# Hybrid decoder layer with 32 experts, one core: gather two tiles ahead at the end of a step, tile loops written out

## What is computed

```python
logits = xf @ w_router + b_router
top_v, top_i = lax.top_k(logits, 4)
gates = softmax(top_v)
# tokens sorted by expert, each expert's rows cut into blocks
hmid = xblk @ w_up[e] + b_up[e]                # 1024 -> 2048
hg = minimum(hmid[:, :1024], 7.0)
hl = clip(hmid[:, 1024:], -7.0, 7.0)
act = hg * sigmoid(1.702 * hg) * (hl + 1.0)
yb = act @ w_down[e] + b_down[e]               # 1024 -> 1024
y = segment_sum(yb * gate, token)
```

## Time and profile before

| what | us |
|---|---|
| median of the runs | 1562.85 |
| the profiled execution, its span | 1565.7 |
| TensorE busy with matmuls | 1300.1 (83%) |
| VectorE busy | 530.9 (34%) |
| ScalarE, GpSimd busy | 209.8, 225.4 |
| share of 16 DMA engines taken by the loads, stores of SyncE's queue | 77.3% |
| weights of the experts | 256 issues of 1024 KB and 256 of 512 KB |

### The profile page before, as it was taken

How to read it: one execution, slowest core, us unless ns; L and a number is a source line. 1 busy time by engine, 2 the same in 40 slices (tenths; PEclk the granted TensorE clock), 3 DMA queues, 4 the chain that set the end, 5 groups by cost and what they waited for, 6 DMA issues and landing times.

```text
span 1565.7 us, 30929 instructions
## 1 busy us (share of the span) xinstructions
PE 1300.1 (83%) x11087; PEld 697.0 (45%) x11088; DVE 530.9 (34%) x1344; ACT 209.8 (13%) x561; POOL 225.4 (14%) x349
## 2 busy tenths in 40 slices
PE   7999999999898977669998996695796886857865
PEld 5778777778786532223443332231232332312322
DVE  2999756643573251111211111111111111111155
ACT  2111232414240210000000000000000000000001
POOL 2008700124220010000100000000010000001320
PEclk9999999999999998779999997898898998978987
DMA  7586455204037789999978999999999999999996
GB/s 186 125 267 158 101 128 143 86 9 109 1 119 230 279 364 419 420 410 416 419 290 357 405 417 418 419 419 416 419 419 417 406 390 412 418 417 419 418 372 237
DMA packets 147329, 480.52 MB, mean 307 GB/s; under 512 B 15438, under 2 KB 76118, under 8 KB 114471
## 3 DMA queue, kind: packets, MB, share of 16 engines
q1 hardware_dynamic: 135695, 463.37, 77.3%
q0 software_dynamic: 2560, 10.29, 1.6%
q10 hardware_dynamic: 9024, 6.17, 1.2%
HBM read 462.42 MB, written 18.21 MB: 307 GB/s over the span
## 4 chain that ended last, share of the span: by engine, by line
PE 59%; DMA 17%; DVE 8%; issue 6%; SPq 3%; POOL 3%; ACT 2%; DVEq 1%; POOLq 0%
PE bank L1287 17%; DMA arena<-in_w_up 16%; PE bank L1299 10%; PE bank L782 9%; PE bank L1255 5%; PE bank L1273 3%; DVE acc L1826 3%; PE bank L1174 2%; PE bank L1182 2%; PE bank L865 2%; POOL acc L548 2%; SPq L447 2%; SPq L450 1%; PE bank L1082 1%; POOL temps L545 1%
## 5 line engine op out<-in xcount | busy, mean ns | idle before, releaser
L1287 PE MATMUL bank<-arena,gate 128*32 128x512 f32 x3264 | 420.0, 643 | 125.4 <-DMA arena<-in_w_up 124.8
L1287 PEld LDWEIGHTS bank<-arena,gate 128*32 128x32 f32 x3264 | 103.9, 113 | 395.8 <-issue 270.7
L782 PE MATMUL bank<-arena 128*128 128x304 f32 (+1 forms) x1024 | 263.9, 420 | 3.7 <-DMA arena<-in_w_in 2.2
L2368 DVE COPY gate<-bank 128x256 f32<-128x256 f32 x46 | 19.6, 425 | 634.9 <-PE bank L1299 634.9
L782 PEld LDWEIGHTS bank<-arena 128*128 128x128 f32 x1024 | 196.9, 193 | 68.2 <-ACT zs L1497 3.1
L1299 PE MATMUL bank<-arena,gate 128*32 128x256 f32 x3264 | 190.5, 384 | 30.9 <-ACT gate L1717 29.3
L1299 PEld LDWEIGHTS bank<-arena,gate 128*32 128x32 f32 x3264 | 112.4, 111 | 96.7 <-issue 27.1
L1826 DVE SCALAR_TENSOR_TENSOR acc<-arena,pcol,acc x240 | 126.3, 609 | 0.1
L672 POOL TENSOR_TENSOR qkv<-qkv 128x192 f32<-128x192 f32 x46 | 29.4, 639 | 613.3 <-DVE qkv L2312 613.3
L1273 PE MATMUL bank<-qkv 128*128 128x512 f32 x102 | 59.5, 666 | 49.9 <-DVE gate L2354 23.4
L1255 PE MATMUL bank<-qkv 128*32 128x256 f32 (+1 forms) x1224 | 87.2, 401 | 2.0 <-POOL qkv L675 1.2
(11 more groups left out here) (424 smaller groups left out, 1169.7 us busy)
## 6 DMA issues: line engine op xcount, KB each, us to landing
arena<-in_w_up SPq DMA_DIRECT2D x256, 1024.0 KB, 12.7
arena<-in_w_down SPq DMA_DIRECT2D x256, 512.0 KB, 8.6
arena<-in_w_in SPq DMA_DIRECT2D x32, 1024.0 KB, 10.4
y_d<-gate ACTq DMA_DIRECT2D x188, 32.0 KB, 4.9
y_d<-gate POOLq DMA_DIRECT2D x1, 4608.0 KB, 28.3
arena<-in_w_conf_out SPq DMA_DIRECT2D x4, 1024.0 KB, 5.1
arena<-in_state_dn_S SPq DMA_DIRECT2D x8, 512.0 KB, 7.3
arena<-in_w_dn_out SPq DMA_DIRECT2D x1, 4096.0 KB, 15.2
```

The lines of the kernel that those rows point to most:

```text
L782: last = mm(bank[2 * (j % 2) + f][:, 0:cols.stop - cols.start], wring[:, slot, k, P * half:P * (half + 1)], rhs[:, k, cols], start=(k == 0 ...
L1287: last = mm(hidden(q)[v], xgT[:, i, SL * q0:SL * (q0 + 1)], parts(wup[k], q)[v], start=False, stop=(k == KC - 1), skip_group_check=True)
```

## The change

- The two halves of bank 0 are taken apart: the turned rows go to the right half of bank 6 (`xgt_bank`), so VectorE reads them there.
- In a step, the gather moves from after up chunks 0 to 3 to the end, and it is that of tile b+2, not b+1. The turn of tile b+1's rows moves from the end to just after the turn of the activation, before down. It gets a wait for `y_ready`. In the last four steps the gather stands at the end too, in the first two of them.
- ScalarE's order becomes `copy_actt(b-1)`, `store_y(b-1)`, `sigmoid(b)`, `copy_xg(b+2)`.
- No loop over tiles stays on TensorE, ScalarE, VectorE and GpSimd. Tiles 2 to 27 are written out, then 35 steps each inside the condition of the one before (`nx > b - FIXED`), then the last four. Tile numbers are constants but in the last four. The gates are now turned before tile 28.
- VectorE no longer makes the table of tile numbers (12 or so small operations). SyncE's loop stays.

```diff
             def tile_step(b):                       # TensorE
                 up_bias(b)
                 up(b, range(0, 4), now_in)
-                gather(b + 1)
                 turn(act_h, bank[4], s["act_ready"], b, s["actt_done"])
+                if not first(prev):
+                    pe.wait_ge(s["y_ready"], prev)
+                turn(xg, xgt_bank, s["xg_copied"], b + 2, s["xgt_done"])
                 down(prev, range(KC), prev_in)
                 up(b, range(4, KC), now_in)
-                turn(xg, bank[0][:, W:2 * W], s["xg_copied"], b + 2, s["xgt_done"])
+                gather(b + 2)
...
-            with pe.Fori(2, HEAD) as b:
+            for b in range(2, FIXED):
                 tile_step(b)
             turn_gates()
             pe.wait_ge(s["mask_ready"], 3)
             nx = pe.value_load(info_i[0:1, 0:1], min_val=0, max_val=XB)
-            with pe.Fori(0, MID) as i:
-                b = pe.value_load(info_i[0:1, bass.ds(i + O_MID, 1)], min_val=0, max_val=XB + MID) + HEAD
-                tile_step(b)
-                with pe.Fori(0, EXTRA) as j:
-                    with pe.If(i + j * MID < nx):
-                        tile_step(b + j + 1)
+            with ExitStack() as more:
+                for b in range(FIXED, FIXED + XB):
+                    more.enter_context(pe.If(nx > b - FIXED))
+                    tile_step(b)
...
             def tile_step(b):                       # ScalarE
-                copy_xg(b + 1)
                 copy_actt(b - 1)
+                store_y(b - 1)
                 sigmoid(b)
-                store_y(b - 1)
+                copy_xg(b + 2)
...
-                if i < LAST - 1:                    # TensorE, the last four
-                    gather(b + 1)
                 turn_choice(i)
                 turn(act_h, bank[4], s["act_ready"], b, s["actt_done"])
+                if i < LAST - 1:
+                    pe.wait_ge(s["y_ready"], prev)
+                    turn(xg, xgt_bank, s["xg_copied"], b + 2, s["xgt_done"])
...
-                if i < LAST - 1:
-                    turn(xg, bank[0][:, W:2 * W], s["xg_copied"], b + 2, s["xgt_done"])
+                if i < LAST - 2:
+                    gather(b + 2)
```

More of the change, by code:

```diff
@@ L168, in build @@
         iota_e = iota_t[:, 0:NE]
-        info_i = small(O_MID + MID, I32)
+        info_i = small(N_INFO, I32)
         brt = small(32)
@@ L1366, in _ @@
             gather(0)
-            turn(xg, bank[0][:, W:2 * W], s["xg_copied"], 1, s["xgt_done"])
+            turn(xg, xgt_bank, s["xg_copied"], 1, s["xgt_done"])
             up_bias(0)
@@ L1371, in _ @@
             up(0, range(4, KC), 16)
-            turn(xg, bank[0][:, W:2 * W], s["xg_copied"], 2, s["xgt_done"])
+            turn(xg, xgt_bank, s["xg_copied"], 2, s["xgt_done"])
             pe.wait_ge(s["tab_ready"], 1)
-            tile_step(1)
-            with pe.Fori(2, HEAD) as b:
+            in1 = landed_for(1)
+            up_bias(1)
+            up(1, range(0, 4), in1)
+            gather(2)
+            turn(act_h, bank[4], s["act_ready"], 1, s["actt_done"])
+            down(0, range(KC), 16)
+            up(1, range(4, KC), in1)
+            pe.wait_ge(s["y_ready"], 1)
+            turn(xg, xgt_bank, s["xg_copied"], 3, s["xgt_done"])
+            gather(3)
+            for b in range(2, FIXED):
                 tile_step(b)
@@ L1737, in _ @@
             sigmoid(0)
-            tile_step(1)
-            with act.Fori(2, HEAD) as b:
+            copy_xg(2)
+            copy_actt(0)
+            store_y(0)
+            sigmoid(1)
+            copy_xg(3)
+            for b in range(2, FIXED):
                 tile_step(b)
             nx = act.value_load(info_i[0:1, 0:1], min_val=0, max_val=XB)
[L1742 to L1747, removed]
+            with ExitStack() as more:
+                for b in range(FIXED, FIXED + XB):
+                    more.enter_context(act.If(nx > b - FIXED))
+                    tile_step(b)
             for i in range(LAST):
                 b = nx + (NE - LAST + i)
-                if i < LAST - 1:
-                    copy_xg(b + 1)
                 act.wait_ge(s["pgt_done"], i + 2)
@@ L2377, in _ @@
             tile_step(1)
-            with dve.Fori(2, HEAD) as b:
+            for b in range(2, FIXED):
                 tile_step(b)
@@ L2382, in _ @@
             nx = dve.value_load(info_i[0:1, 0:1], min_val=0, max_val=XB)
-            with dve.Fori(0, MID) as i:
-                b = dve.value_load(info_i[0:1, bass.ds(i + O_MID, 1)], min_val=0, max_val=XB + MID) + HEAD
-                tile_step(b)
-                with dve.Fori(0, EXTRA) as j:
-                    with dve.If(i + j * MID < nx):
-                        tile_step(b + j + 1)
+            with ExitStack() as more:
+                for b in range(FIXED, FIXED + XB):
+                    more.enter_context(dve.If(nx > b - FIXED))
+                    tile_step(b)
             def add_tile(i, c, out):
```

39 lines of the change are left out of this document (11 added, 28 removed).

## The result

The changed kernel takes 1579.06 us (median of 4 runs, 1578.03 to 1579.96), beside 1562.44 for the kernel before on the same chip: a ratio of 1.0099, 95% interval 1.008 to 1.0118 (the ratio on record; the two medians divide to 1.0106). So it is slower by 1.0%, where I had forecast 0.5% faster. The profiled execution has a span of 1576.5 us, 10.8 more than before.

The account below looks back on a forecast made before the run. The DMA engines' limit of about 418 GB/s bounds the expert half, so only dips can be won: gains 12.4 less losses 5.2 take the span from 1565.7 to 1558.5, predicted median 1555.7 us, range 1549 to 1566.

Parts of the forecast that it names:

- The step: TensorE's work for one tile without waits: the new order shortens it by 0.94 to 14.17 us.
- A and B: DMA dips at 800 to 840 (expert 8) and 840 to 870 us (pause before tile 16): gains of 2 and 6.1 us.
- C: DMA dip at 1250 to 1300 us, from the pause before tile 37: gain of 4.3 us as table reads go.
- Fetched code: Instruction fetches for 45 more written-out tiles, 67 packets on the DMA engines: loss of 4.2 us.
- rival 1: Fetched code stalls the weights, each packet costing up to its full 1 us: slower, up to 1618 us; chance 0.20.
- rival 2: Pauses return as conditions or code pages cost TensorE 2 us or more a step: no change, 1562 us; chance 0.17.
- rival 3: Code costs nothing and the end loses nothing, all 12.4 us kept: 1550.4 us; chance 0.13.
- The end: Last four tiles, with the moved gather waiting for late `pmat` and a jump over unused copies: loss of 1 us (-2 to +5).
- the slack in it takes most of the 5.3: Tile 48's up starts 7.3 us after up of step 47 instead of 2.0, mostly absorbed by step 48's wait for `take_y`.
- The jump: Branch over 16 unused step copies before the last four tiles: a new pause of 0.8 to 5 us.

Follow-up runs that it names:

- after: The changed kernel itself, against the kernel before: 1579.06 us, ratio 1.0099.
- before_loops: The kernel before, own order kept, with two plain loops in place of its first loop and the nested ones, no table: 1553.59 us, ratio 0.9938.
- all_loops: The changed kernel with its written-out tiles and nested conditions replaced by two plain loops on all four engines: 1558.8 us, ratio 0.9971.
- order_only: The changed kernel's new order of the step and end, with the loops and table of the kernel before: 1579.96 us, ratio 1.0083.
- same_after: The changed kernel run once more, unchanged: 1582.55 us.
- match_first: all_loops with VectorE doing match before activate in the last steps: 1552.31 us, ratio 0.9910.
- unused_code: The kernel before plus copies of a step behind each engine's last instruction, under a run-time condition false for this input: 1576.74 us, ratio 1.0057.
- after_tail: The changed kernel with the old order in the last steps, the jump over unused copies kept: 1576.16 us, ratio 1.0061.
- pe_written: The changed kernel with TensorE still written out and the other three engines in loops: 1585.56 us, ratio 1.0115.
- unroll_only: The kernel before, in its old order, with the changed kernel's written-out tiles and nested conditions: 1578.51 us, ratio 1.0075.

## Why the prediction was wrong, point by point

- **The step, right.** Two biases without a wait between them stand at 819.87 and 833.86 in after: 13.99 us, forecast 14.17, before 15.1.
- **A and B, right in kind, too large.** Forecast 2 + 6.1, measured 6.5. before_loops has 5.4 of it with the old order, so the order gave about 1, not 2, and B gave nearly its 6.1.
- **C, right, in part by luck.** Forecast 4.3, measured 4.4. But two more profiles of the kernel before lost only 1.1 and 2.0 there, so the gain is mostly smaller. I took one profile's dip for a fixed one.
- **Fetched code, right as far as levels given to 1 GB/s can say.** 56 packets more in 560 to 1570 (forecast 63). Their bytes are 2.2 us and the plain stretches lost 1.9 more: 4.1, forecast 4.2. Against all_loops, with the same order and the code in loops, the plain stretches lost 2.8 more. But order_only lost 3.7 and before_loops 2.5 there without one packet more, so not all of it need be the fetches. The level stayed at 416 and above (415 in one stretch of same_after), so rival 1 did not happen, and neither did rival 2 (no pauses in the steps) nor rival 3.
- **The end, wrong.** The step that failed is "the slack in it takes most of the 5.3". The lateness of the gather was right (forecast 4.7, measured 4.72), but it isn't absorbed: taking it away alone gives 5 to 9 us (match_first against all_loops). I had compared it with `take_y` of tile 47 and its wait for the stores; but the next expert's up can be issued only when tile 48's step has used the chunks, and that step stands behind the gather. The jump, put at 0.8 to 5, was 6.52, and I gave it no price of its own. I also left out that each pause is followed by work on the lower clock level. In all the term is 10.3 where I wrote 1 (-2 to +5). I had named a loss above 5 as the thing that would make the prediction wrong.
- **What had no term.** The start, 7.2 us. I took for granted that code that isn't changed takes the same time. unused_code shows what the size alone costs: 1.0057, some 9 us, with nothing of the added code run.

Forecast span 1558.5, measured 1576.5: 18.0 apart. The points give 7.2 (start) + 9.3 (end) + 1.6 (A and B), less 0.2 (C and code): 17.9. Of the readings of the rows one was off and changes nothing: the slices reach 420 GB/s, not 421. The split between the causes at the end, the gather, the jump and the stutter, stays open to some 3 us each.

The late start alone would have turned the forecast of 7.2 us of gain into no change. A rival "slower" was there with 0.20, but its mechanism, the fetches, was not the one that came.

The Trainium skill, in "Runtime: NRT & Kernel Launch", section "Instruction fetch mechanics", says that a taken branch out of the present window has to wait for its page, and gives that as one reason to write code out in full where possible. The first half agrees with the 6.52 us at the jump over unused copies: from 1450 to 1458 two packets pass in the instruction queue. The advice does not hold for this kernel: written out it is 1.0099, as two plain loops 0.9971 with the same order, and the plain loops' rounds show no pause.

## What to carry to other kernels

Count a larger program as a cost of its own, to parts that the change doesn't touch as well: compare the DMA engines' share at equal GB/s in an untouched stretch. A plain loop with a bound read at run time gave all that the written-out code gave here; what had cost stood at the outer rounds of the nest, with their table read and their skipped copies, not in looping as such. And when an operation moves ahead in an engine's order, follow its input back to the engine that makes it in every special case, the written-out last steps above all, and take slack off the price only when the chain to the next transfer's issue has been read to its end.

## What the runs showed of the hardware

- The packets of 1 KB in the mixer took 56 to 66 ns with little code for TensorE and 88 to 97 with much, 97 with none of the added code run (unused_code). The expert half's level was 415 to 419 GB/s in both in most stretches.
- The way over 16 unused copies of a step on TensorE took 6.5 us in after, same_after, after_tail and pe_written (4.9 in unroll_only), and an outer round of the nested loops 2.4 to 3.8 (order_only), with a table read and one or two skipped copies in it. A read of a number at run time with no loop beside it stood at a pause of 2.7 (after). The round of a plain loop took nothing that shows.
- Fetched code cost the weights an estimated 4 to 5 us for 56 packets of 16 KB, of which the bytes are 2.2; the rest is worked out from levels given to 1 GB/s.
- Beside GpSimd's indirect fetches, TensorE ran in 11 of 16 executions in pieces of about five matmuls, 1.45 us apart, from about 7 us after the first fetch. It varies from one execution of a program to the next.
